# Local attention's last steps reordered, and the first output projection by rows with half of it ahead of the delta mixer

## The reference

```python
def ab_mixer(u, w_in, conv_w, a_log, dt_bias, a_out_g, bq_g, bk_g, sink, w_out):
    proj = u @ w_in
    qa, ka, va, za, ba, aa, qb, kb, vb = split_cols(proj, AB_SIZES)
    ya = delta_mixer(qa, ka, va, za, ba, aa, conv_w, a_log, dt_bias, a_out_g)
    qb = rmsnorm(qb.reshape(bsz, n, B_HEADS, B_HD), bq_g) * (B_HD ** -0.5)
    kb = rmsnorm(kb.reshape(bsz, n, B_KV, B_HD), bk_g)
    yb = window_mixer(qb, kb, vb, sink)
    return jnp.concatenate([ya, yb.astype(ya.dtype)], axis=-1) @ w_out
...
def delta_mixer(hq, hk, hv, hz, hb, ha, conv_w, a_log, dt_bias, o_gain):
    qkv = jax.nn.silu(centred_conv(jnp.concatenate([hq, hk, hv], axis=-1), conv_w))
    q = l2norm(q) * (A_DK ** -0.5); k = l2norm(k)          # 4 heads of 128
    beta = sigmoid(hb); g = -exp(a_log) * softplus(ha + dt_bias)
    o = fwd + bwd             # gated delta rule, both directions
    return rmsnorm(o, o_gain) * silu(hz)
```

## Time and profile before

| | us |
|---|---|
| three runs, median | 1615.46 (1614.97 to 1618.35) |
| profiled execution | 1608.75 |
| its span | 1606.7 |
| TensorE busy | 1549.6 (96%) |
| VectorE busy | 1112.0 (69%) |
| ScalarE busy | 790.4 (49%) |
| mean granted TensorE clock | 0.984 of 2.4 GHz |

### The profile page before, as it was taken

One profiled execution on the slowest core, in us unless ns is written; L12 is line 12 of the kernel. 1 busy time (PEld: TensorE's weight loads), 2 busy tenths in 40 slices (PEclk: granted clock), 3 DMA queues, 4 the chain that ended last, 5 costly groups with the idle time before them and its releaser, 6 DMA issues.

```text
span 1606.7 us, 32152 instructions
## 1 busy us (share of the span) xinstructions
PE 1549.6 (96%) x12948; PEld 1491.2 (93%) x12948; DVE 1112.0 (69%) x2018; ACT 790.4 (49%) x1368; POOL 179.7 (11%) x200
## 2 busy tenths in 40 slices
PE   7987899999999999999999999999999999999997
PEld 6875898999999799999998899999999999999997
DVE  5884555776777767777868665776767666666666
ACT  4537225443454654444744565544455546554443
POOL 2690201000021020000100102000020001100000
PEclk9999698999999999999999999999999999999999
DMA  6321002444545045454534433656455355255551
GB/s 216 140 71 53 1 3 91 172 157 179 186 160 191 28 158 203 164 209 162 188 124 157 158 107 122 203 175 201 167 170 183 121 190 177 77 186 184 184 196 67
DMA packets 125816, 236.33 MB, mean 147 GB/s; under 512 B 2615, under 2 KB 50026, under 8 KB 125690
## 3 DMA queue, kind: packets, MB, share of 16 engines
q1 hardware_dynamic: 124201, 230.24, 41.1%
q0 software_dynamic: 1296, 4.26, 0.9%
q10 hardware_dynamic: 192, 0.05, 0.0%
HBM read 233.49 MB, written 1.05 MB: 146 GB/s over the span
## 4 chain that ended last, share of the span: by engine, by line
PE 85%; DVE 8%; issue 2%; ACT 2%; DMA 1%; POOL 1%; ACTq 0%; DVEq 0%; POOLq 0%
PE ps L632 49%; PE ps L679 6%; PE ps L678 6%; PE ps L677 6%; PE ps L640 5%; PE ps L822 2%; DVE w_lo L2298 2%; PE ps L783 1%; PE ps L728 1%; DVE hidden L2349 1%; PE ps L763 1%; DVE mx L2654 1%; PE ps L796 1%; ACT w_hi L1626 1%; POOL square_sum L3283 1%
## 5 line engine op out<-in xcount | busy, mean ns | idle before, releaser
L1626 ACT ACTIVATE w_hi<-raw 128x1024 fp32r<-128x1024 f32 x440 | 461.0, 1051 | 277.0 <-PE ps L679 135.7
L2298 DVE TENSOR_TENSOR w_lo<-raw,w_hi 128x1024 fp32r<-128x1024 f32 x440 | 544.8, 1238 | 9.4 <-ACT w_hi L1626 9.4
L632 PE MATMUL ps<-u_hi,w_hi 128*128 128x256 f32 (+1 forms) x1480 | 427.6, 289 | 3.0 <-issue 1.2
L632 PE MATMUL ps<-u_hi,w_lo 128*128 128x256 f32 (+1 forms) x1480 | 421.4, 285 | 0.0
L632 PE MATMUL ps<-u_lo,w_hi 128*128 128x256 f32 (+1 forms) x1480 | 420.9, 284 | 0.0
L632 PEld LDWEIGHTS ps<-u_hi,w_hi 128*128 128x128 f32 x1480 | 281.1, 190 | 8.1 <-issue 4.5
L632 PEld LDWEIGHTS ps<-u_hi,w_lo 128*128 128x128 f32 x1480 | 281.2, 190 | 0.0
L632 PEld LDWEIGHTS ps<-u_lo,w_hi 128*128 128x128 f32 x1480 | 280.2, 189 | 0.6
L632 PE MATMUL ps<-a_hi,w_hi 128*128 128x256 f32 (+1 forms) x864 | 247.4, 286 | 1.0 <-DVE a_lo L2313 0.4
L632 PE MATMUL ps<-a_lo,w_hi 128*128 128x256 f32 (+1 forms) x864 | 244.6, 283 | 0.0
L632 PE MATMUL ps<-a_hi,w_lo 128*128 128x256 f32 (+1 forms) x864 | 244.5, 283 | 0.0
(11 more groups left out here) (426 smaller groups left out, 2242.4 us busy)
## 6 DMA issues: line engine op xcount, KB each, us to landing
raw<-in_w_ff_dram SPq DMA_DIRECT2D x32, 2048.0 KB, 7.7
raw<-in_ffn_w_gu_dram SPq DMA_DIRECT2D x44, 1024.0 KB, 7.0
raw<-in_ffn_w_down_dram SPq DMA_DIRECT2D x10, 2048.0 KB, 7.7
raw<-in_xa_w_kv_dram SPq DMA_DIRECT2D x8, 2048.0 KB, 7.9
raw<-in_od_w_in_dram SPq DMA_DIRECT2D x6, 2048.0 KB, 7.7
raw<-in_w_in_ab_dram SPq DMA_DIRECT2D x5, 2048.0 KB, 7.7
raw<-in_ev_w_in_dram SPq DMA_DIRECT2D x5, 2048.0 KB, 7.7
raw<-in_xa_w_q_dram SPq DMA_DIRECT2D x4, 2048.0 KB, 7.9
```

Of the source, the lines that this page charges most:

```text
L632: mm = pe.matmul(bank[:, 0:n], wx[:, q, k * P:(k + 1) * P], x[ux][:, k, ts], start=k == 0 and i == 0, stop=k == KD - 1 and i == 2)
L1626: act.activation(quarter(w_hi, b, q), raw_quarter(b, q), ACT.Copy).then_inc(high_split, 1)
L2298: dve.tensor_tensor(quarter(w_lo, b, q), raw_quarter(b, q), quarter(w_hi, b, q).bitcast(F32), ALU.subtract)\
```

## The change

Four things. (1) The gate tiles 12 and 13 go from steps 10 and 11 to step 13, 14 and 15 from steps 12 and 13 to step 18, behind the turns; ACT's and DVE's splits of the blocks involved follow. (2) The norms: keys first, queries second, each with its own buffer for squares and scales; ACT squares both at step 13; DVE multiplies at steps 15 and 16; turns three a step at 16 and 17. (3) `w_out_ab` is loaded by rows, as two wide blocks, the attention's rows first. Its eight tiles of 12 matmuls (`window_part`) are no longer behind the mixer: four are in the preparation, all in bank `ps6`, four between the head norms' sums; DVE adds each (`add_part`). The second block, the mixer's rows, is a `block_wide`. (4) Preparation: r0's and r1's rows and keys come first, ahead of the wait for the last attention result; the key products, equal for both directions of a piece, are made twice and not four times; the two 16-token chains share bank `ps7` and wait in pairs.

```diff
-    add("ab_out", [[cols(w["w_out_ab"][0], c)] for c in (0, BLOCK)])
+    add("ab_out", [[(None, 0, x[rows:rows + BLOCK].rearrange("(k p) n -> p k n", p=P))] for rows in (BLOCK, 0)])
...
+        GATE_TILES = {13: (12, 13), 18: (14, 15)}
-        delta_sq, delta_r = area(work, 0, 4, T), area(work, 4 * T, 4, T)
+        delta_sq = {KEYS: area(work, 0, 4, T), QUERIES: area(mx, 9952, 4, T)}
-        PREPARED = FIRST + CHAINS
-        CHAIN_BANKS = dict(zip(CHAINS, ((tile_bank[0], tile_bank[1]), (tile_bank[2], tile_bank[3]), (b4, b5), (b6, b7))))
+        PREPARED = CHAINS[0:2] + FIRST + CHAINS[2:]
+        CHAIN_BANKS = dict(zip(CHAINS, ((tile_bank[0], tile_bank[1]), (tile_bank[2], tile_bank[3]), (b4, b6), (b5, b7))))
+        KEY_BANKS = {2: tile_bank[1], 1: tile_bank[3]}
+        EARLY_PARTS = 4
...
+            def window_part(t):
+                b = first_of("ab_out")
+                if t % 2 == 0:
+                    split_ready(b, t // 2)
+                if t <= EARLY_PARTS:
+                    pe.wait_ge(tile_read, tile_at[b] + t)
+                bank = part_bank(t)
...
+                for k in range(4):
+                    pe.matmul(bank[:, 0:T], hi[:, k, cols], a_hi[:, 4 + k], start=k == 0, stop=False)
+                    pe.matmul(bank[:, 0:T], hi[:, k, cols], a_lo[:, 4 + k], start=False, stop=False)
+                    mm = pe.matmul(bank[:, 0:T], lo[:, k, cols], a_hi[:, 4 + k], start=False, stop=k == 3)
+                mm.then_inc(tile_summed, 1)
             def gated_delta():
                 pe.wait_ge(M["d_copied"], 6)
+                pe.wait_ge(M["d_normed"], 2)
+                pe.wait_ge(tile_read, tile_at[first_of("ab_out")])
+                delta_rows(r0)
+                delta_rows(r1)
+                delta_keys(r0)
+                delta_keys(r1)
                 pe.wait_ge(operand_split, window_ready)
                 for chain in FIRST:
                     delta_first(chain)
-                delta_rows(r0)
-                delta_rows(r1)
+                window_part(0)
+                delta_rows(r2)
+                delta_queries(r0)
                 first_turn()
-                delta_queries(r0)
+                window_part(1)
...
             gated_delta()
-            head_norms([(1, T, ones)] * 4)
-            out_product("ab_out", full, chunks_ready(4) + [window_ready] * 4)
+            head_norms([(1, T, ones)] * 4, between=lambda i: window_part(EARLY_PARTS + i))
+            op[0] += 4
+            block_wide(first_of("ab_out") + 1, 0, 4, full, op[0] - 4)
...
             # ScalarE, attention's steps
-                if k < 15:
+                if k < 11:
                     split_high(ab + 1 + (k + 1) // 4, (k + 1) % 4)
+                if k in (16, 17, 20, 21):
+                    split_high(ab + 4, (16, 17, 20, 21).index(k))
...
+                    for which in (KEYS, QUERIES):
+                        act.activation(delta_sq[which], delta_heads[which], ACT.Square).then_inc(M["d_sq"], 1)
...
             # VectorE
+            def add_part(k):
+                gt = tile_at[out_block] + k
+                dve.wait_ge(tile_summed, gt + 1)
+                dve.wait_ge(tile_read, gt)
+                dve.tensor_tensor(hidden[:, k], part_bank(k)[:, 0:T], hidden[:, k], ALU.add).then_inc(tile_read, 1)
...
+            split_low(out_block, 3)
             for d in range(2):
                 dve.wait_ge(M["d_s"], d + 1)
                 dve.tensor_copy(state[:, d], by_head(S_BANKS[d][:])).then_inc(M["d_s_read"], 1)
+                split_low(out_block + 1, d)
...
-                       gate=[za[:, h] for h in range(4)], ts=full)
-            residual("ab_out", "mlp0", full)
+                       gate=[za[:, h] for h in range(4)], ts=full, fill=lambda i: add_part(EARLY_PARTS + i))
+            split_low(out_block + 1, 2)
+            down(out_block + 1, full, "mlp0")
```

More of the change, by code:

```diff
@@ L984, in chain_w @@
                 if level == 1:
-                    pe.wait_ge(M["d_n"], prepared(chain))
+                    pe.wait_ge(M["d_n"], products_order(chain))
                 if level == TOP:
@@ L2021, in _ @@
                         ins.then_inc(M["d_x5"], 1)
+            out_block = phases["ab_out"].first
+            for q in range(2):
+                split_high(out_block + 1, q)
             for i, chain in enumerate(KEY_NORMS):
@@ L2414, in head_norms @@
                         gates(i)
+                        if fill is not None:
+                            fill(i)
                         if between is not None:
@@ L2693, in window_step @@
             def window_step(k):
-                if k < 15:
+                if k < 11:
                     qkvz_step(1 + k)
+                if k == 11:
+                    split_low(ab + 3, 3)
+                for n in GATE_TILES.get(k - 1, ()):
+                    scaled(za[:, n - 12], n % 4, tile_at[ab] + n, full)
             def conv_step(k):
```

189 lines of the change are left out of this document (111 added, 78 removed).

## The result

The changed kernel took 1602.53 us (median of 4 executions, 1601.24 to 1605.35) beside 1615.22 us for the kernel before on the same chip: ratio 0.9937, interval 0.9921 to 0.9953, so 8 to 13 us faster, where 17.5 was forecast. The profiled execution took 1603.22 us with a span of 1601.4, only 5.3 us shorter than the span of before; the median fell by 12.7.

A forecast was written before the change was run, and what follows sets the result against it. TensorE, busy 96%, was taken as the bound, losing time only where its queue stands still or its clock is low. +1.5 - 6.5 - 0.7 - 12.0 = -17.7 us from 1615.46 gives 1597.8, say 1598 us; 8-in-10 range 1590 to 1610.

The forecast's parts named there:

- Norms and projection: First norm sum to last add: 20.8 us instead of 32.8, so -12.0; at low clock throughout the norms 29.3 (-3.5).
- the 2.2 us of idle between the sums: Norms before the projection: the share of the -12.0 us put down to TensorE's idle between the norm sums.
- Preparation: Delta mixer's preparation: 25.0 us instead of 31.5, so -6.5; bounds 22 us (-9.5) and 38.5 at low clock (+7.0).
- VectorE's 21.0 us: Preparation: VectorE's work, 19.24 us plus four adds of 0.44; the stage was chosen near this bound, with 4 us of waits.
- My 21.6 us of PE work: Preparation: TensorE's own work at full clock, summed over products, 16-token chains and four half tiles; 38.5 us at low clock.
- The other reason: Preparation: the half tiles make the stage dense, and the granted clock came back in dense stretches.
- Attention's tail: Attention's last steps: 55 us against 53.5, taken as +1.5 us, from -3 to +5.
- 9.35 - 6 + 8: Attention's last steps, TensorE's idle: 9.35 us now, 6 removed by earlier silu and reordered norms, 8 added by emptied and unfilled steps.
- 1.2 for a short low clock after the new idle: Attention's last steps: 1.2 us added to TensorE's work of 44.15 us, for low clock behind the emptied steps.
- The first level and the values: After the preparation: first level's products, now 3.15 us at low clock, gain 0.7; levels and values otherwise keep their length.
- The offset: Whole kernel: the median's 6.7 us above the profiled execution, carried over unchanged, so 1591.0 us profiled became a median of 1597.8.
- The signs named: What the changed profile would show: idle near 116 to 121 us, then slower products; stage times, clocks and shifts.

The follow-up runs named there:

- old gate tiles: The changed kernel with gate tiles 12 to 15 put back in steps 10 to 13, all else still changed: 1593.48 us, ratio 0.9876 to the kernel before.
- spread: The changed kernel with the gate tiles in steps 11, 12, 19 and 20, one a step: 1594.49 us, ratio 0.9883 to the kernel before.
- first profile: The kernel before, unedited, in the profile on which the prediction rested: profiled execution 1608.75 us, span 1606.7 us.
- second profile: The kernel before, unedited, profiled again: profiled execution 1615.9 us, span 1614.0 us.
- the repeat: The changed kernel, unedited, timed and profiled again: 1600.93 us, ratio 0.9927 to the kernel before.
- tiles in 11, 12, 13 and 19: The changed kernel with the four gate tiles in steps 11, 12, 13 and 19: 1591.75 us, ratio 0.9857 to the kernel before.

## Why the prediction was right, and where it was off

**The sign and the two large terms held.** Norms and projection: forecast 20.8 us to the start of the last add, measured 21.3 where the clock was 1.00 (old gate tiles) and 23.8 in the changed kernel; so -8.9 and not -12.0. The work was counted right but for 0.5 us; the term that failed is the clock of 1.00: the norms run low from 250.8 to 257.6, as they did from 251.2 before. Why they do so in one profile and not in another stays open. Among the causes given for the -12.0, the 2.2 us of idle between the sums were too many: before, PE's waits from the first sum on were 0.90, 0.20 and 0.43 us, 1.5 in all. Preparation: forecast 25.0 us, measured 25.2 at clock 1.00 (spread) and 26.5 in the changed kernel; -5.6 against the first profile, not -6.5. The reason given, that VectorE's 21.0 us are nearly the bound, was wrong although VectorE's busy time came out at 21.5: PE is busy 24.8 of 26.5 us. My 21.6 us of PE work were too few; even at 1.00 it is 23.5 (spread). The other reason, that the half tiles bring the full clock back, held: without them it is 0.50 in the stage's last 8 us.

**Attention's tail was mis-sized: +1.5 forecast, +5.1 measured in the windows.** In its own terms: idle was to be 9.35 - 6 + 8 = 11.35 us, and was 12.0; work 43.65, and was 46.6. The idle sum came out by two errors, which is luck. The new order of the norms saves about 2 us of idle (to the end of the meta values, where the table's tail ends, it was 8.7 to 9.5 us in the three profiles before and is 6.9 with the old gate tiles), not 6, for the silu hardly moved. The emptied steps cost 5.2, not 8. The work term failed by the clock: "1.2 for a short low clock after the new idle" was 13.4 us of low clock at 117.7 to 131.1, and the meta step did not run at full (3.69 us, not 1.7 less than 3.42). The old gate tiles show that this is no net price of the emptied steps: with them the tail's work is 47.4 us, not less, its low clock lies at the end instead, and all that the tail wins is idle. The rule of the Trainium skill that the prediction cites (TensorE: Matmul & The Clock Gate, section HAM oscillation) has a wait between bursts of matmuls take the clock down again. This trace agrees: the clock is low from 117.4 us, behind the wait of 1.50, and step 12's values take 1.70 us behind that of 4.80. Tile 12 did start at 1.2 GHz, and the tail lay at the upper end of the range given for it (+5), even a little past it.

**The first level and the values** were to gain 0.7 us and lost 0.7: they began at low clock, until 199.4. With clock 1.00 they take 54.3 us, 1.1 less than before.

**The offset.** The forecast carried 6.7 us from the first profile to the median unchanged. That surplus was real, and in the second profile it was low clock in the tail of before, a stage that the change alters. The changed kernel has no such surplus: its median is 0.7 us under its profiled execution. Without the 6.7 us the sum gives 1591 for that execution, and it took 1603.2, so the sum of the stages was off by 12 us; that the forecast of the median was off by only 5 is in good part luck. Against the first profile the norm product of the MLP, which stands behind the projection, came 7.4 us earlier (281.1 for 288.5): step 10's start +1.3, tail +5.7, preparation -5.65, levels and values +0.65, norms and projection -8.9, behind it -0.5. Against the second profile (295.6) it is -14.5. The measured medians, -12.7 here and -11.9 in the repeat, lie between. Behind that product little changed: 1320.3 and 1317.9 us in the two profiles of the changed kernel, 1318.2, 1318.4 and 1318.4 in the three before.

**The signs named.** Right: the idle in steps 11 and 12 with slow products behind it, the preparation at a clock over 0.9; at the edge, VectorE idle there 5.0 us (under 5 was forecast). Wrong: silu 2 us earlier, the end of attention within 3 us (it is 7.0 later), the levels' end 6 to 7 us earlier (the values' end is 2.0 later), clock 1.00 in the norms, 17 to 18 us at the MLP (7.4 against that profile).

**Not settled.** Whether old gate tiles or tiles in 11, 12, 13 and 19 are better, and why a low stretch comes at a given place in one execution and not in the next. The norms' new order, the halved key products and the projection by rows were not timed alone; what the new order of chains gives the total is not known either.

## What to carry to other kernels

Where TensorE is nearly always busy, an edit that takes filling work away from steps that wait for another engine is paid in idle, here 5 us: TensorE only reaches the wait sooner. Keep work that has to be done in such steps, even at the cost of its place elsewhere; products without use there gave back 1 us of clock and nothing in the total. Wide products between groups of small ones can pay for themselves by the clock that they hold up, as in the preparation. Count a stage's work at full clock and once more at the clock that the trace shows, and take a second profile of the kernel before when its profiled execution lies off the median: one stage may hold the whole difference. Compare stages between the same instructions, and not between the same microseconds. When two places ask for the same filling tile, try both, since the gain of one place may come out as a low stretch at another.
